# Routing an expert-choice layer per token, from the raw residual, while the last projection of the mixer still runs

## The reference, cut to what matters

```python
x_new = x + g1 * ox                      # ox: last projection of the mixer, @ w_out
x_new = x_new + g2 * expert_choice_ffn(modulate(x_new, norm2_g, sh2, sc2), ...)

def modulate(x, g, shift, scale):
    y = x * rsqrt(mean(x * x, -1) + EPS) * g
    return y * (1.0 + scale) + shift

def expert_choice_ffn(h, w_router, w_gate, w_up, w_down):
    aff = softmax(h @ w_router)                      # 256 tokens x 16 experts
    g, idx = top_k(aff.transpose(0, 2, 1), cap)      # cap = 32
    xs = h[idx]
    y = (silu(xs @ w_gate) * (xs @ w_up)) @ w_down   # per expert, 1024 x 1024 each
    return zeros.at[idx].add(y * g)
```

## Time and profile before

| | us |
|---|---|
| median of 3 runs | 2346.15 (2341.69 to 2349.91) |
| the profiled execution | 2350.06 |
| its span, first to last instruction | 2348.7 |
| PE busy | 1900.9 |
| DVE busy | 958.9 |
| ACT busy | 696.5 |

### The profile page before, as it was taken

One profiled execution on the slowest core, in us unless ns is written; L12 is line 12 of the kernel. 1 busy time (PEld: TensorE's weight loads), 2 busy tenths in 40 slices (PEclk: granted clock), 3 DMA queues, 4 the chain that ended last, 5 costly groups with the idle time before them and its releaser, 6 DMA issues.

```text
span 2348.7 us, 29995 instructions
## 1 busy us (share of the span) xinstructions
PE 1900.9 (81%) x13150; PEld 1355.9 (58%) x13150; DVE 958.9 (41%) x1667; ACT 696.5 (30%) x1129; POOL 4.1 (0%) x11
## 2 busy tenths in 40 slices
PE   7699999888898999698958888888868666665656
PEld 5489999778777999675733323333355533232323
DVE  5766655666655665844460101010164501010101
ACT  5345544553524444534331000000144300000000
POOL 0000000000000000000000000000000000000000
PEclk9899999899998999799979999999989788787778
DMA  6664445432466445311319999999912399999997
GB/s 260 234 241 160 175 148 214 152 145 72 177 254 255 180 146 198 117 31 68 132 48 396 428 427 428 428 428 427 399 42 100 144 390 427 427 427 427 427 427 322
DMA packets 44786, 606.52 MB, mean 258 GB/s; under 512 B 5104, under 2 KB 5232, under 8 KB 6768
## 3 DMA queue, kind: packets, MB, share of 16 engines
q1 hardware_dynamic: 43488, 597.61, 63.0%
q0 software_dynamic: 880, 4.98, 0.6%
q10 hardware_dynamic: 288, 2.02, 0.2%
HBM read 603.54 MB, written 1.05 MB: 257 GB/s over the span
## 4 chain that ended last, share of the span: by engine, by line
PE 51%; DMA 27%; DVE 14%; ACT 6%; issue 2%; SPq 0%; DVEq 0%; ACTq 0%
PE ps L86 49%; DMA m_last_slot<-moe_down 16%; DMA m_more<-moe_up 10%; DVE m_WL L95 2%; ACT m_WH L92 1%; PE ps L89 1%; ACT m_mix_sc L92 1%; DVE m_od_low L101 1%; DMA m_ring<-ev_in 1%; DVE m_misc L104 1%; DVE m_wk L95 1%; ACT L92 1%; DVE m_ev L95 1%; DVE m_mix_sc L95 1%; DVE m_misc L113 0%
## 5 line engine op out<-in xcount | busy, mean ns | idle before, releaser
L86 PE MATMUL ps<-m_ring,m_moe_sc 128*32 128x256 f32 (+1 forms) x2304 | 418.4, 547 | 80.3 <-DMA m_ring<-moe_gate 74.8
L95 DVE TENSOR_TENSOR m_WL<-m_ring,m_WH 128x1024 fp32r<-128x1024 f32 (+1 forms) x277 | 329.7, 1202 | 270.9 <-ACT m_WH L92 270.2
L92 ACT ACTIVATE m_WH<-m_ring 128x1024 fp32r<-128x1024 f32 (+1 forms) x277 | 282.3, 1034 | 137.5 <-PE ps L86 123.1
L86 PEld LDWEIGHTS ps<-m_ring,m_moe_sc 128*32 128x32 f32 (+1 forms) x2304 | 154.7, 143 | 228.6 <-issue 122.4
L86 PE MATMUL ps<-m_more,m_moe_sc 128*32 128x256 f32 (+1 forms) x768 | 210.7, 561 | 83.2 <-DMA m_more<-moe_up 83.2
L86 PE MATMUL ps<-m_nH,m_WH 128*128 128x256 f32 x936 | 236.9, 289 | 18.3 <-ACT m_WH L92 18.3
L95 DVE TENSOR_TENSOR m_nT<-ps,m_nT 128x512 f32<-128x512 f32 (+1 forms) x32 | 17.9, 558 | 556.2 <-PE ps L86 556.2
L86 PE MATMUL ps<-m_nL,m_WH 128*128 128x256 f32 x936 | 236.9, 289 | 9.0 <-DVE m_nL L101 8.9
L92 ACT ACTIVATE m_nT<-ps 128x512 f32<-128x512 f32 (+1 forms) x64 | 31.4, 490 | 620.6 <-PE ps L89 326.1
L86 PE MATMUL ps<-m_last_slot,m_nT 128*32 128x256 f32 (+1 forms) x768 | 187.6, 502 | 30.2 <-DMA m_last_slot<-moe_down 30.2
L86 PE MATMUL ps<-m_more,m_nT 128*32 128x256 f32 (+1 forms) x768 | 190.7, 503 | 18.6 <-ACT m_nT L92 18.6
(11 more groups left out here) (308 smaller groups left out, 2999.4 us busy)
## 6 DMA issues: line engine op xcount, KB each, us to landing
m_ring<-moe_gate SPq DMA_DIRECT2D x64, 2048.0 KB, 19.0
m_ring<-moe_up SPq DMA_DIRECT2D x32, 2048.0 KB, 17.6
m_more<-moe_up SPq DMA_DIRECT2D x32, 2048.0 KB, 22.3
m_more<-moe_down SPq DMA_DIRECT2D x32, 2048.0 KB, 18.0
m_last_slot<-moe_down SPq DMA_DIRECT2D x32, 2048.0 KB, 22.6
m_ring<-ada SPq DMA_DIRECT2D x24, 2048.0 KB, 8.1
m_ring<-ffn_down SPq DMA_DIRECT2D x16, 1408.0 KB, 5.9
m_ring<-ffn_gate SPq DMA_DIRECT2D x10, 2048.0 KB, 7.9
```

Source lines behind the costliest of these rows:

```text
L86: return Issued() if self.dry else self.e.matmul(out, lhsT, rhs, start=start, stop=stop, skip_group_check=skip)
L92: return Issued() if self.dry else self.e.activation(*a, **k)
L95: return Issued() if self.dry else self.e.tensor_tensor(*a)
```

## The change

Four things change.

1. The router works on the raw residual. `dve_router` folds the norm gain and (1 + scale) into the router's weights (`wrs`) during the mixer, `pe_shift_logits` computes what the shift adds to the logits. After each tile of the last projection, PE multiplies the tile before it, as stationary operand, with 16 columns of `wrs`, and its squares with one column of ones (`pe_tokens_of_tile`); both accumulate over the tiles in one bank. So logits and sums of squares come out with tokens on the partitions. The normed tensor `n2` is no longer made.
2. Both sides are chosen together: 16 or 32 rows in one set of DVE instructions.
3. The norm is applied later: the token's factor `r4` when the rows are split, the gain, scale and shift when `xs` is copied out of PSUM. `rows` and `hot` have a buffer for each side. `Pg` and its transposes move behind the gather, the transposes between expert 0's up projection and its `aT`.
4. Slots 3, 4 and 5 wait for the inputs of the last projection instead (`mixed`).

```diff
+        routed = small[:, OFF["levels"][0]:OFF["levels"][0] + 512]
+        wrs = routed[:, 0:256].rearrange("p (s k n) -> p s k n", s=2, k=8)
+        by_shift = routed[:, 256:288].rearrange("p (s n) -> p s n", s=2)
+        lg, aff = routed[:, 288:352], routed[:, 352:416]
+        r4, st = routed[:, 416:420], routed[:, 420:440]
+        sq_tok = [wk[:, i * 256:(i + 1) * 256] for i in range(4)]
+        router = lambda l: sm("w_router", 128 * l, 128 * l + 128).rearrange("p (k n) -> p k n", k=8)
...
+        def dve_router(l):
+            for s in range(sides_of[l]):
+                g, dst = sm("n2", 8 * l, 8 * l + 8), s1[:, 16 + 8 * s:24 + 8 * s]
+                dve.tensor_scalar(dst, mod(l, 4, s), 1.0, None, ALU.add).then_inc(*V.mark())
+                dve.wait_ge(*V.now()).tensor_tensor(dst, dst, g, ALU.mult).then_inc(*V.mark())
+                dve.wait_ge(*V.now()).tensor_tensor(wrs[:, s, :, :], router(l), bc(dst.unsqueeze(2), [128, 8, 16]), ALU.mult).then_inc(*V.mark(("wrs", l)))
+        def dve_shift_logits(l):
+            n = sides_of[l]
+            dve.wait_ge(*at(("shift logits", l)))
+            dve.tensor_copy(by_shift[:, 0:n, :], bank["shift logits", l][:, 0:16 * n].rearrange("p (s n) -> p s n", s=n)).then_inc(
+                *V.mark(("shift logits out", l)))
+        def pe_shift_logits(l):
+            ps, before = bg.take(("shift logits", l), ("shift logits out", l))
+            pe.wait_ge(*before)
+            for s in range(sides_of[l]):
+                for k in range(8):
+                    ins = pe.matmul(ps[:, 16 * s:16 * s + 16], bc(mod(l, 3, s)[:, k:k + 1], [128, 128]), router(l)[:, k, :], k == 0, k == 7)
+            ins.then_inc(*P.mark(("shift logits", l)))
+        def pe_tokens_of_tile(l, j):
+            n = sides_of[l]
+            if j == 0:
+                ps, before = bg.take(("logits", l), ("logits out", l))
+                pe.wait_ge(*before).wait_ge(*at(("wrs", l)))
+            ps = bank["logits", l]
+            for s in range(n):
+                pe.wait_ge(*at(("x", ("mix", l), s, j)))
+                for t in range(2):
+                    o = 16 * (t * n + s)
+                    pe.matmul(ps[:, o:o + 16], src[s][:, j, t * 128:(t + 1) * 128], wrs[:, s, j, :], j == s == t == 0, False, True)
+                pe.wait_ge(*at(("sq", ("mix", l), s, j)))
+                for t in range(2):
+                    o = 64 + t * n + s
+                    ins = pe.matmul(ps[:, o:o + 1], sq_tok[(n * j + s) % 4][:, t * 128:(t + 1) * 128], ones[:, 0:1], False, j == 7 and s == n - 1 and t == 1, True)
+                ins.then_inc(*P.mark(("by token", l, s, j)))
...
-            run(pe_dense(("m_out", l), "w_out", (l,), list(range(8)), 8, lambda q: m2H[:, q, 0:nside, :], lambda q: m2L[:, q, 0:nside, :],
-                         ready("H"), ready("L"), fg, per=1, width=256 * nside))
+            pe_shift_logits(l)
+            j = 0
+            for _ in pe_dense(("m_out", l), "w_out", (l,), list(range(8)), 8, lambda q: m2H[:, q, 0:nside, :], lambda q: m2L[:, q, 0:nside, :],
+                              ready("H"), ready("L"), fg, per=1, width=256 * nside):
+                if j:
+                    pe_tokens_of_tile(l, j - 1)
+                j += 1
+            pe_tokens_of_tile(l, 7)
...
+                if j == 7:
+                    act.activation(junk[:, 0:1], sm("eps"), ACT.Sqrt).then_inc(*A.mark())
                 for s in range(nside):
-                    act_square(("mix", l), src[s], j, 1, s, ("x", ("mix", l), s, j))
+                    act.wait_ge(*at(("x", ("mix", l), s, j)))
+                    u = nside * j + s
+                    if u >= 4:
+                        act.wait_ge(*at(("by token", l, (u - 4) % nside, (u - 4) // nside)))
+                    act.activation(sq_tok[u % 4], src[s][:, j, :], ACT.Square).then_inc(*A.mark(("sq", ("mix", l), s, j)))
...
+            dve_router(l)
...
-            pending = []
+            dve_shift_logits(l)
...
-                    for s_, j_ in pending:
-                        dve_square(("mix", l), j_, 1, s_)
-                    pending[:] = [(s, j)]
...
+        by_tokens = lambda a: a[:, :].rearrange("p (t f) -> p t f", t=2)
+        rowsH = [by_tokens(sb("rowsH0", 2048, F32R, offset=r_base + 4 * 11376)), by_tokens(sb("rowsH1", 2048, F32R, offset=r_base + 4 * 8192))]
+        rowsL = [by_tokens(sb("rowsL0", 2048, F32R, offset=r_base + 4 * 13424)), by_tokens(sb("rowsL1", 2048, F32R, offset=wk_place))]
+        hot = [sb("hot0", 1024, F32R, offset=r_base + 4 * 27760)[:, :], sb("hot1", 1024, F32R, offset=r_base + 4 * 10240)[:, :]]
...
+            last = nside - 1
+            mixed = (("mfL", l, last), ("mpL", l, last), ("mvL", l, last, 3))
+            W.begin([0, 1, 2, 3, 4, 5], {3: mixed, 4: mixed, 5: mixed})
+            R = 16 * nside
+            def rows(side, some):
+                for n in some:
+                    t, hf = n // 2, n % 2
+                    pe_transposes(("rows", l, side, n), [src[side][:, hf * 4 + i, t * 128:(t + 1) * 128] for i in range(4)],
+                                  [("x", ("mix", l), side, hf * 4 + 3)], bg, ("rowsL", l, side, n))
+            rows(0, range(4))
+            ps, before = fg.take(("affT", l), ("affT out", l))
+            pe.wait_ge(*before).wait_ge(*at(("aff", l)))
+            for t in range(2):
+                ins = pe.transpose(ps[0:R, t * 128:(t + 1) * 128], aff[:, R * t:R * t + R], ident)
+            ins.then_inc(*P.mark(("affT", l)))
+            ps, before = fg.take(("places", l), ("hot", l, last))
+            pe.wait_ge(*before).wait_ge(*at(("cs", l)))
+            for t in range(2):
+                ins = pe.transpose(ps[:, t * R:(t + 1) * R], cs[0:R, t * 128:(t + 1) * 128], ident[0:R, 0:R])
+            ins.then_inc(*P.mark(("places", l)))
+            if nside > 1:
+                rows(1, range(4))
...
+                if e == 0:
+                    for s in range(nside):
+                        for t in range(2):
+                            pe_transposes(("PgT", l, s, t), [Pg_of[s][:, t * 512 + i * 128:t * 512 + (i + 1) * 128] for i in range(4)], [("Pg", l, s)],
+                                          fg, ("PgT out", l, s, t))
...
+            n = 2 * nside
+            act.wait_ge(*at(("by token", l, nside - 1, 7)))
+            act.activation(r4[:, 0:n], bank["logits", l][:, 64:64 + n], ACT.Sqrt, bias=sm("eps"), scale=1.0 / D).then_inc(*A.mark(("token root", l)))
+            act.activation(junk[:, 0:1], sm("eps"), ACT.Exp).then_inc(*A.mark())
+            act.wait_ge(*at(("lg", l)))
+            act.activation(aff[:, 0:16 * n], lg[:, 0:16 * n], ACT.Exp).then_inc(*A.mark(("aff exp", l)))
-                act_root(("moe", l, side), rooms[side], table=side == 0)
+                for i in range(4):
+                    t, hf = i // 2, i % 2
+                    act.wait_ge(*at(("rows", l, side, i))).wait_ge(*at(("token norm", l)))
+                    act.activation(rowsH[side][:, t, hf * 512:(hf + 1) * 512], bank["rows", l, side, i][:, :], ACT.Copy,
+                                   scale=r4[:, t * nside + side:t * nside + side + 1]).then_inc(*A.mark(("rowsH", l, side, i)))
...
+                    act.wait_ge(*at(("xs", l, side, k)))
+                    act.activation(xs[:, k, :, side, :], bank["xs", l, side, k][:, :].rearrange("p (e n) -> p e n", e=16), ACT.Identity,
+                                   bias=mod(l, 3, side)[:, k:k + 1], scale=s1[:, 16 + 8 * side + k:17 + 8 * side + k]).then_inc(*A.mark(("xs out", l, side, k)))
...
+                if e == 0:
+                    for s in range(nside):
+                        for t in range(2):
+                            d = PgT[:, s, :, t * 128:(t + 1) * 128]
+                            act_copy(d, turned(("PgT", l, s, t), d), [("PgT", l, s, t)], ("PgT out", l, s, t))
...
+            n, R = 2 * nside, 16 * nside
+            rows16 = lambda a: a[:, 0:16 * n].rearrange("p (g e) -> p g e", g=n)
+            dve.wait_ge(*at(("token root", l))).reciprocal(r4[:, 0:n], r4[:, 0:n]).then_inc(*V.mark(("token norm", l)))
+            dve.wait_ge(*V.now())
+            for t in range(2):
+                for s in range(nside):
+                    i = t * nside + s
+                    dve.scalar_tensor_tensor(lg[:, 16 * i:16 * i + 16], bank["logits", l][:, 16 * i:16 * i + 16], r4[:, i:i + 1], by_shift[:, s, :],
+                                             ALU.mult, ALU.add).then_inc(*V.mark(("logits out", l)))
+            dve.wait_ge(*V.now()).tensor_reduce(st[:, 0:n], rows16(lg), AX.X, ALU.max).then_inc(*V.mark())
+            dve.wait_ge(*V.now()).tensor_tensor(rows16(lg), rows16(lg), bc(st[:, 0:n].unsqueeze(2), [128, n, 16]), ALU.subtract).then_inc(*V.mark(("lg", l)))
...
+            dve.wait_ge(*at(("aff exp", l))).tensor_reduce(st[:, 0:n], rows16(aff), AX.X, ALU.add).then_inc(*V.mark())
+            dve.wait_ge(*V.now()).reciprocal(st[:, 0:n], st[:, 0:n]).then_inc(*V.mark())
```

(31 more changed lines are left out.)

173 lines of the change are left out of this document (13 added, 160 removed).

## The result

| | us |
|---|---|
| before, median of 4, measured beside it | 2345.62 (2341.69 to 2349.91) |
| changed kernel, median of 4 | 2312.65 (2310.0 to 2319.11) |
| ratio, with its 95% interval | 0.9863 (0.9836 to 0.989) |
| the profiled execution of the changed kernel, its span | 2319.11, 2317.8 |

A forecast was written before the change was run, and what follows sets the result against it. Each layer's DMA-full stretch from expert 0 on was taken as fixed, so only time ahead of it counts. Savings of 20.5 us (layer 0) and 8.1 (layer 1), 28.6 together, gave 2346.15 - 28.6 = 2317.5 us, range 2306 to 2330.

The forecast's parts named there:

- The bound: From expert 0 on, a DMA-full stretch of fixed length per layer; each microsecond ahead of it moves the kernel's end by one.
- Short matmuls: Small matmuls of tiles 0 to 5 inside the last projection: 0.223 us each, adding 10.7 us in layer 0, 5.4 in layer 1.
- The shift's logits: Small matmuls ahead of the last projection: 0.9 us added in layer 0, at most 3.6; layer 1 0, at most 1.8.
- Chooser and gather: From the last projection's end to expert 0: 33.7 us in layer 0, was 65.8; 24.6 in layer 1, was 38.1.
- its two terms: Layer 0's gather: side 0 at 8.8 us including 1.0 for a colder start, side 1 with expert 0's start at 8.6.
- The table load: ACT's switch from root to exponential, 1.28 us, hides beside DVE work in the chooser, without the skill's 1.4 us more per layer.
- Slot 5: Its earlier weight load ahead of the DMA-full stretch brings no more than a fraction of a us.
- the third rival: Around expert 0, the gain doesn't reach the end: DMA hole or growth, or slow gathers; up to 15 us lost; 7%.
- Doubled short matmuls: Rival: small matmuls in projections cost about double, 0.45 us; 21 us more, time 2338.5; 8%.
- A slow clock in the projections: Rival: small matmuls taken for idleness, dense matmuls of both projections lose half their pace; 61 us, end near 2379; 4%.
- A hole in the DMA share: Rival: DMA stretch from expert 0 starts with a hole as late down slots stall it; 2330 to 2336; 7% with its variants.
- More saved: Rival: shorter handovers, gather warm from the start, shift's logits wholly hidden; another 5 to 12 us, under 2306; 6%.

The follow-up runs named there:

- e11: The changed kernel again with no edit, measured beside two kernels with extra matmuls; 2316.67 us, ratio to before 0.9857.
- e5: Changed kernel with the affinities' copy and four chooser rounds run a second time on a scratch copy, interleaved; 2320.22 us, ratio to before 0.9881.
- e2: Changed kernel with the shift's logits computed inside the attention, between its units, instead of ahead of the projection; 2316.63 us, ratio to before 0.9867.
- e10: Changed kernel with both edits of e9 and e2 together; 2310.77 us, ratio to before 0.9842.
- e9: Changed kernel with 25 extra 512-column matmuls during DVE's rounds and 13 more ahead of layer 1's gather; 2313.67 us, ratio to before 0.9852.
- e1: Changed kernel with slots 3 and 4 waiting for the last residual tile again, slot 5 for the gather's end; 2315.12 us, ratio to before 0.9867.
- e8: Changed kernel with 12 extra 512-column matmuls during DVE's rounds and eight more ahead of layer 1's gather; 2310.93 us, ratio to before 0.9851.

## Why the prediction was right

**The bound** was read rightly. What a stretch ahead of expert 0 gains or loses reaches the end in full: from the start of layer 0's projection to the end it is 1192.7 us in e11 (2306.1 - 1113.4) and 1199.4 in e5 (2316.5 - 1117.1), 6.7 more where the stretches have 6.6.

**Short matmuls.** A tile took 5.44 us and takes 7.27: 1.83 for eight, 0.229 each against 0.223 forecast. Six tiles are 11.0 us. In layer 1 a tile takes 3.77 instead of 2.87, so six are 5.4, as forecast, yet the projection grew by 3.8 only: before, its granted clock was 0.93, and after it is 1.00, a gift of 1.5 us that was not in the sum. It is luck of the executions: PE waits at the same places in e2 and e10, and there the clock stays up.

**The shift's logits** were the term that was off in layer 0: 0.9 forecast, 2.1 measured (e2). Behind this row the projection starts 4.6 us after the 64-row matmuls (1113.42 to 1118.03, e11); by then the kernel before had run nine of the projection's matmuls (1122.54 to 1125.98), not four, and 9 x 0.23 is 2.1. It lay within the bound of 3.6. In layer 1 they cost nothing, as taken.

**Chooser and gather** came out at 33.0 us in e11 (1172.85 to 1205.88) and 34.3 in the first profile, against 33.7; in layer 1 at 23.7 against 24.6. 32 rows cost what 16 do. The gather of layer 0 was 0.5 us shorter than its two terms; the reason given for its extra 1.0, a colder start, is only half of it: e9 shows DVE's work for side 1 as a second bound of nearly the same length. The prediction counted four banks free for the gather's first groups; one of them holds the places until side 1's matrix is there, so it was three.

**The table load** hid as taken: 1.28 us, and the real exponential starts 0.16 us behind its end, most of it the dummy's. By the rule of the Trainium skill ("ScalarE: Activation LUTs", "What ACT_TABLE_LOAD costs") it would have been 1.4 us later; this case doesn't show that drain. No second load came behind the squares.

**Slot 5** was wrong in layer 1. The prediction judged it by layer 0, where the chunk is over in time; in layer 1 expert 0 frees its first slot 4.4 us behind that chunk's issue, and the early load takes 1.0 us off the DMA stretch (e1). The stretch is 1.8 us shorter than before (449.3 - 447.5); the rest stays open.

**The sum.** Layer 0: 112.1 - 92.5 = 19.6 us (20.5 forecast; 16.8 in the first profile, where the clock took 2.8 us). Layer 1: 65.7 - 55.2 = 10.5 (8.1). The DMA stretch of layer 1: 1.8 (0). Together 31.9, against 28.6. The medians differ by 33.0 in the first measurement and 30.9 with e11. So the mechanism held, and the close agreement of the total is in part luck: the shift's logits were 1.2 us too cheap, the two choosers with their gathers 0.7 and 0.9 us too dear, and the 1.5 us of clock and the 1.8 of the DMA stretch were not foreseen. The stated range does not follow from its own bounds either: 5 and 2.7 us down and 7, 7.5 and 2.8 up give 2310 to 2335, where it says 2306 to 2330, and the 15 us of the third rival end at 2332.5, not 2336. One reading is off as well: the matmul behind the eight small ones starts 0.14 us ahead of their last end (508.25 against 508.39), not within 0.04.

**The rivals.** Doubled short matmuls: refuted by 0.229 us. A slow clock in the projections: the dense matmuls ran slowly for some 3.3 us in two profiles of twelve, 1.6 us lost each time, nowhere near 61. A hole in the DMA share: none, 1.00 over 436 and 447 us. More saved: 4.9 us by the median, short of what this rival named, and not for its reasons: the gather did not start warm, and the shift's logits were not hidden in layer 0.

**The clock.** In the first profile it fell in the middle of the tail. Changed kernel, busy time by stretch:

```profile
1185.00:1186.00 1.00, 1.00 (x11) 1.00 (x10) 0.00 (x0) 0.00 (x0) 0.00 (x0) 0.95 0.92 393
1186.00:1187.00 1.00, 1.00 (x7) 1.00 (x6) 0.00 (x0) 0.00 (x0) 0.00 (x0) 0.50 1.12 475
```

PE is busy throughout, but only with matmuls of 1 and 16 columns; at 1186 it is granted 1.2 GHz. The same happened in e2 and e10, with PE just as busy; in the nine other profiles the tail ran at the full clock to its end, and the 16 transposes took 2.07 us instead of 3.65. It is worth 1.2 us in the chooser (17.4 against 16.2). The Trainium skill ("TensorE: Matmul & The Clock Gate", "What's actually happening") has activity release the throttle and says that the number of slow matmuls at a kernel's start varies from run to run. That it varies within a kernel too, the traces show (none, or 7 and 8 at the projection's start); why the clock should fall under a PE that is never idle, no run here tells.

## What to carry to other kernels

When one resource runs full from some point on, only the time until that point counts; look which of its requests are still open when the stretch starts, in each layer anew. Work that used to need a finished tensor (norm sums, router logits) can often be accumulated tile by tile in token order while the tensor is made; the price is one short matmul more per piece (0.23 us here, whether 1 or 16 columns), to be taken from a row, and it pays where a chain of dependent small steps disappears. Before you warm an engine up or speed its first steps, look whether another engine's wait lies right beneath them, and which results still hold the banks that it will want. When work moves into a stretch that looks idle, measure that stretch too (0.4 us in e2).

## What the runs showed of the hardware that I had not expected

- MAX8 and MATCH_REPLACE8 on 256 elements take 0.42 and 0.40 us on 16 partitions and on 32. Two independent MAX8 behind one another take 0.74 together, not 0.84 (e5).
- Copies with a scale (and bias) per partition cost more than plain ones: a 128x512 copy from PSUM took 0.78 us on ACT and 0.81 on DVE, where a plain one took ACT 0.60 (`m_m2H`) and DVE 0.69 (the copies of `xs` in the kernel before).
- With PE kept busy on 512-column matmuls through DVE's rounds the 2.4 GHz level stayed (e9, granted clock 1.00 to the end of the gather); with half of them and then 3.1 us of idle PE it was lost (e8, 0.50 behind the idle stretch).
- PE's clock fell to 1.2 GHz while it worked without a gap on matmuls of 1 and 16 columns, in 3 of 12 profiles.
